# Two groups of TensorE transposes moved in a routed expert loop: gathered rows ahead of the last plain piece, gated rows behind the next turn's gate pieces

## What is computed

```python
combine = jnp.sum(jax.nn.one_hot(expert_id, N_EXPERTS) * weights[..., None], axis=1)   # 2 of 16 experts a token
for e in range(N_EXPERTS):
    he = jax.nn.silu(ht @ w_gate[e]) * (ht @ w_up[e])        # 1024 -> 512
    y = y + combine[:, e:e + 1] * (he @ w_down[e])           # 512 -> 1024
```

## Time and profile before

| | us |
|---|---|
| three runs of the kernel, median (lowest to highest) | 787.44 (785.16 to 789.09) |
| the profiled execution, its time | 787.38 |
| the profiled execution, its span | 785.5 |
| TensorE busy with matmuls | 751.7 |
| VectorE busy | 537.3 |
| ScalarE busy | 456.9 |
| GpSimd busy | 179.9 |

### The profile page before, as it was taken

The page is one execution under the profiler, slowest core; times in us unless marked ns, Lnnn a source line. Parts: engine busy times, 40 slices in busy tenths (PEclk is TensorE's granted clock), DMA queues, the critical chain, the costliest instruction groups (busy, mean ns, idle before and its releaser), DMA issues.

```text
span 785.5 us, 11565 instructions
## 1 busy us (share of the span) xinstructions
PE 751.7 (96%) x4124; PEld 582.1 (74%) x4124; DVE 537.3 (68%) x711; ACT 456.9 (58%) x665; POOL 179.9 (23%) x185
## 2 busy tenths in 40 slices
PE   4999999999999999999999969999999999999994
PEld 3978789777788889888788844677777777777763
DVE  5445378598782455622555488599989889899986
ACT  4455662487883236433443242587887887787862
POOL 3800023000001011000000100135555444555312
PEclk9999999999999999999999989999999999999997
DMA  9934521000405435542104768999999999999942
GB/s 297 233 94 141 155 83 59 1 2 2 161 3 188 134 108 177 172 151 66 53 1 143 310 236 321 398 380 381 383 370 373 382 372 375 380 384 384 385 154 107
DMA packets 61902, 166.88 MB, mean 212 GB/s; under 512 B 8224, under 2 KB 36192, under 8 KB 49576
## 3 DMA queue, kind: packets, MB, share of 16 engines
q1 hardware_dynamic: 56376, 150.69, 51.8%
q0 software_dynamic: 4480, 12.48, 6.8%
q10 hardware_dynamic: 1008, 3.21, 1.2%
HBM read 153.44 MB, written 12.85 MB: 212 GB/s over the span
## 4 chain that ended last, share of the span: by engine, by line
PE 93%; DVE 3%; DMA 1%; ACT 1%; issue 1%; POOL 0%; SPq 0%; POOLq 0%; ACTq 0%; DVEq 0%
PE ps L1976 24%; PE ps L1978 23%; PE ps L1977 23%; PE ps L2249 3%; PE ps L2197 3%; PE ps L2175 2%; PE ps L2444 2%; PE ps L2287 2%; PE ps L2178 1%; PE ps L2108 1%; PE ps L2424 1%; PE ps L2366 1%; DMA raw<-in_w_in 1%; PE ps L2179 1%; PE ps L2430 1%
## 5 line engine op out<-in xcount | busy, mean ns | idle before, releaser
L1356 DVE TENSOR_TENSOR wlo<-raw,whi 128x2048 fp32r<-128x2048 f32 x29 | 66.5, 2292 | 78.5 <-ACT whi L878 78.4
L1976 PE MATMUL ps<-whi,mhi 128*96 128x512 f32 (+1 forms) x276 | 110.1, 399 | 2.0 <-DVE mlo L1909 1.2
L1978 PE MATMUL ps<-whi,mlo 128*96 128x512 f32 (+1 forms) x276 | 109.3, 396 | 0.0
L1977 PE MATMUL ps<-wlo,mhi 128*96 128x512 f32 (+1 forms) x276 | 108.8, 394 | 0.0
L1371 DVE TENSOR_TENSOR wlo<-arena,whi 128x2048 fp32r<-128x2048 f32 x39 | 89.4, 2291 | 20.4 <-ACT whi L897 20.4
L741 POOL TENSOR_SCALAR stat<-stat 128x1 f32<-128x1 f32 x18 | 11.3, 630 | 355.9 <-ACT tok L903 209.4
L897 ACT ACTIVATE whi<-arena 128x2048 fp32r<-128x2048 f32 x39 | 74.7, 1915 | 26.4 <-PE ps L1978 26.4
L878 ACT ACTIVATE whi<-raw 128x2048 fp32r<-128x2048 f32 x29 | 55.4, 1910 | 48.5 <-PE ps L1978 48.4
L1976 PE MATMUL ps<-ahi,whi 128*128 128x512 f32 x192 | 75.6, 394 | 0.0
L1978 PE MATMUL ps<-ahi,wlo 128*128 128x512 f32 x192 | 74.8, 390 | 0.0
L1977 PE MATMUL ps<-alo,whi 128*128 128x512 f32 x192 | 74.8, 390 | 0.0
(11 more groups left out here) (396 smaller groups left out, 1692.4 us busy)
## 6 DMA issues: line engine op xcount, KB each, us to landing
arena<-in_exp_w_gate SPq DMA_DIRECT2D x30, 1024.0 KB, 14.4
arena<-in_exp_w_up SPq DMA_DIRECT2D x17, 1024.0 KB, 14.2
raw_a<-in_exp_w_down SPq DMA_DIRECT2D x16, 1024.0 KB, 15.2
raw<-in_exp_w_up SPq DMA_DIRECT2D x15, 1024.0 KB, 13.3
arena<-in_exp_w_down SPq DMA_DIRECT2D x9, 1024.0 KB, 18.6
raw<-in_exp_w_down SPq DMA_DIRECT2D x7, 1024.0 KB, 15.1
raw<-in_w_in SPq DMA_DIRECT2D x5, 1024.0 KB, 7.3
raw<-in_w_in SPq DMA_DIRECT2D x10, 512.0 KB, 5.6
```

What stands on the lines that cost most here:

```text
L1356: v.tensor_tensor(wlo[:, n % SPLIT, :], raw[:, n % RAW, :], whi[:, n % SPLIT, :].bitcast(F32), ALU.subtract).then_inc(lo_done, 1)
L1976: mm(out_, ahi_, bhi_, start=first, stop=False)
L1977: mm(out_, ahi_, blo_, start=False, stop=False)
L1978: return mm(out_, alo_, bhi_, start=False, stop=last)
```

## The change

On TensorE the row transposes of the entry stand ahead of plain piece 3, and those of the gated rows leave the entry and the end of the turn: they are issued behind the two gate pieces of the next turn, and once more behind the last turn. ScalarE's and VectorE's copies of the gated rows move with them, behind split 7 of the next turn, and in the entry VectorE's low copy of the rows goes ahead of `gated`.

```diff
@@ ScalarE, entry and turn @@
             xg_hi_out(2)
-            he_hi_out(1)
             act.wait_ge(route_done, 1)
...
                 split_expert(at + 7, h)
+                he_hi_out(j)
                 split_expert(at + 8, h)
                 silu(base + 2, j + 1)
...
                     y_out_half(1, base + 6)
-                if not last:
-                    he_hi_out(j + 1)
@@ VectorE, entry and turn @@
             split_expert(6)
+            xg_lo_out(2)
             gated(1, 4)
-            xg_lo_out(2)
-            he_lo_out(1)
             dve.wait_ge(route_done, 1)
...
-                for m in (7, 8, 9, 10):
+                split_expert(at + 7, h)
+                he_lo_out(j)
+                for m in (8, 9, 10):
                     split_expert(at + m, h)
                 gated(j + 1, RING * h + (at + 8), j)
...
                     split_expert(at + 12, h)
-                    he_lo_out(j + 1)
@@ TensorE, entry @@
                 pe.wait_ge(first_in, min(m, 1) + 1)
+                if m == 3:
+                    pe.wait_ge(xg_in, 16)
+                    xg_transposes()
...
-            pe.wait_ge(xg_in, 16)
-            xg_transposes()
-            pe.wait_ge(he_done, 2)
-            he_transposes()
             pe.wait_ge(route_done, 1)
@@ TensorE, turn and behind the last turn @@
                 pe.wait_ge(he_done, j + 1)
+                he_transposes()
                 for m in range(2):
                     pe.wait_ge(lo_done, n0 + 2 + m)
                     in_piece(ps[1], 6 + m, m)
...
                     down_piece(8 + m, m, 4)
-                pe.wait_ge(he_done, j + 2)
-                he_transposes()
...
             turn(turns + 1, True)
+            pe.wait_ge(he_done, turns + 3)
+            he_transposes()
             pe.wait_ge(he_lo, turns + 2)
```

## The result

The changed kernel takes 788.86 us (median of 22 runs, 787.89 to 790.29), the kernel before 787.70 on the same chips (22 runs, 785.16 to 789.19). The ratio is 1.002, 95% interval 1.0012 to 1.0028: the change makes the kernel 0.2% slower. The profiled execution took 789.06 us around a span of 787.2 (before: 787.38 and 785.5). The times of the kernel before fall into two groups with nothing between them: 6 of the 22 runs lie at 785.16 to 785.57 and the others at 787.18 to 789.19. In the runs beside the experiments the lower group has a mean granted clock of 0.991 and the upper one 0.987 to 0.989. Only one execution, of the upper group, has a trace, so which stop of the clock the lower group is spared is not shown. The changed kernel's 22 runs form one group.

The account below looks back on a forecast made before the run. TensorE, never idle in the expert loop, was taken as the bound, with idle stretches only at its entry. Entry gain -3.58 and loop loss +4.95 gave +1.37 us on 787.4: 788.7 us, range 784.0 to 791.2.

Parts of the forecast that it names:

- Gather's wait, row transposes, piece 3: Entry: wait of some 0.3 us, transposes 0.67, piece 3.44; first turn starts at 492.21, gain 3.58 us.
- Register load and branch code under piece 3, at nothing: Entry: TensorE's sequencer code ahead of the loop can run under piece 3's matmuls, costing nothing; bound above 0.47 us.
- Clock at full speed from turn 1 on: Entry: first gate piece runs at full clock, taking 2.84 us instead of 4.41.
- Rival C: Start of turn 1: clock stays at half speed, costing 1.57 us; 790.3 us; chance 0.08.
- Part 3, 15 x 0.33 = +4.95: Loop: moved gated-row transposes lengthen each of 15 turns by 0.33 us, while the boundary saving becomes a wait; 4.95 us lost.
- Rival A: Turn boundaries: wait hidden, turns keep 17.66 us, only the last turn's 0.33 lost; about 784.1 us; chance 0.14.
- ScalarE's copy between splits 7 and 8 is hidden: Turns: 0.49 us copy makes split 9 late by at most 0.1; 0.86 us idle ahead of split 10 covers it.
- rival B: ScalarE's queue in turns: the copy delays silu and later splits; 0.3 us more each gives 793.3 us; chance 0.09.
- The gather lands in time: Entry: first gather lands at 488.02, 5.4 us after issue; second near 499.5, ahead of its use at about 503.7.
- rival D: Entry: gather late or register code uncovered, giving 2 us instead of 3.6; 790.3 us; chance 0.09.
- The weights' pace (E): Loop: pace of weight loads, not TensorE, takes over; some 11 us of lead left late; no chance of its own.
- Behind the last turn, no change: End of the last turn: old order of down pieces, transposes and two copies, with 1.25 us of waiting, stays.

Follow-up runs that it names:

- experiment 3: Kernel before, with only the entry's row transposes ahead of plain piece 3 and their copy ahead of the gated multiply; 788.88 us, ratio 1.0007.
- experiment 5: Kernel before, with one instead of four transposes in each group of the gated rows; 787.91 us, ratio 1.0005.
- experiment 7: Kernel before, with TensorE's register load of the number of turns and its wait moved ahead of plain piece 3; 785.34 us, ratio 0.9977.
- experiment 4: Changed kernel, with the entry's row transposes behind plain piece 3 again, leaving only the loop's part; 790.34 us, ratio 1.0037 to the kernel before.
- experiment 1: Changed kernel, with VectorE's low copy of the gathered rows ahead of the gated multiply in every turn; 784.65 us, ratio 0.9962 to the kernel before.
- experiment 6: Changed kernel, with one instead of four transposes in each group of the gated rows; 784.43 us, ratio 0.9963 to the kernel before.
- Experiment 8: Changed kernel, low copy ahead of the gated multiply, entry's row transposes behind the first quarter of plain piece 3; 784.11 us, ratio 0.9956 to the kernel before.
- experiment 2: Kernel before, with VectorE's low copy of the gathered rows ahead of the gated multiply; 796.28 us, ratio 1.0117.

## Why the prediction was right

The forecast was 788.7 us, +1.37 on the profiled execution; measured was 788.86, +1.16 between medians and +1.18 by the account. Both terms came out smaller than forecast, the gain by 0.21 us and the loss by 0.40, and the two errors partly cancel. That the total is met to 0.2 us is in part luck; that each term is met to a tenth of its size or better is not. By its own steps:

- **Gather's wait, row transposes, piece 3** (-3.58 us as a sum): 3.37 were gained. The wait was 0.39 us for 0.3. The piece ended up 3.03 us long and not 3.44 (489.58 to 492.61), and the missing 0.4 came back on the first gate matmul, whose step is 0.64 us. The gate piece that was put at 2.84 us (its working, eleven steps of 0.23 and one of 0.29, gives 2.82) therefore took 3.17. The sum holds to 0.2 us, the terms less well.
- **Register load and branch code under piece 3, at nothing.** Turn 1's first matmul follows piece 3 with no idle time, so the code lies covered. But the prediction read the 0.73 us gap as the wait for the low copy, with at most 0.47 us for code behind it. Experiments 3, 5 and 7 show the code as what ended it: without the copy in the way the gap is 0.77 us, with a shorter group turn 1 starts no sooner, and without the register load the copy alone would have held it for 0.38. The bound of 0.47 holds only while the copy waits beside the code. The prediction reached the right sum because both go away together, which is luck in this term; the forecast of experiment 3, on the same reading, went wrong.
- **Clock at full speed from turn 1 on.** Right: 1.00. Rival C is out for the profiled execution. The Trainium skill (TensorE: Matmul & The Clock Gate, "Part 4: PE-mode transpose") says that transposes don't count as TensorE activity as matmuls do. By that rule an entry with a stop and eight transposes in it could have gone to half speed; the row shows 1.00. The runs don't refute the rule either: the stops that did cost clock were longer, 0.90 + 0.73 us before, 0.90 + 0.99 in experiment 5 and 1.19 + 0.77 in experiment 3, each around the gated group, and the 1.39 us of experiment 4 and 0.90 + 0.38 of experiment 7 cost none. Between the kernel before and experiment 7, a third of a microsecond of idle time at this place decided on 1.6 us. Each of these is one profiled execution.
- **Part 3, 15 x 0.33 = +4.95.** The mechanism is right, and shown by experiments 1, 5 and 6. The size is 4.55, because the price at a boundary was put too high. A turn of experiment 1, which has the group and no wait, lasts 17.67 us, and one of the changed kernel, which has both, 17.97. So what the boundary wait costs with its restart is 0.30 and not the 0.33 of the group that it replaces, and the group's own price is lost only in the last turn: 14 x 0.30 + 0.33 = 4.53. Rival A was on the right spot, and its turns of 17.66 us are what experiment 1 has (17.67) once the copy ends early enough.
- **ScalarE's copy between splits 7 and 8 is hidden.** Split 10 still has 0.86 us of idle time ahead of it (738.25): rival B is out.
- **The gather lands in time**: 5.6 us behind its issue; rival D is out for this execution. But its first half is near: in the profiled execution of experiment 1 the gather took 6.1 us, and TensorE waited 0.89 us for it. Experiment 8 has a later point, at which its execution shows no wait.
- **The weights' pace (E)** never released a split in the rows read; the gaps of the chain are named TensorE and ScalarE as before.
- **Behind the last turn, no change**: 1.25 us, as before.

Left open: how much of experiment 2's extra 0.3 us a turn is branch code and how much is wait handling, and why its two boundaries differ by 0.15 us. An experiment without that code would need the loop unrolled and wasn't made. Open too is which stop of the clock the lower group of the kernel before is spared, since no execution of that group was profiled.

## What to carry to other kernels

Work that stands in front of a held wait is free there as long as it ends first, and moving it costs nearly its full price (here 0.30 of 0.33 us) unless the wait moves as well: first ask which release the next step really hangs on and what is queued ahead of that on the releasing engine. Here one exchange in VectorE's queue, copy ahead of multiply, turned a change of +0.2% into one of -0.4%, and the same exchange without the change cost 1.2%, because then the multiply was the one that TensorE stood for: the two orders belong together. Keep register loads away from the place behind a wait that is held, and look there for other sequencer code, such as a loop's branch.

## What the runs showed of the hardware

- The first split matmul directly behind plain f32 matmuls has a step of 0.63 to 0.64 us to the next (492.61 to 493.25, and 492.53 to 493.16 in experiment 8), where one behind transposes has 0.28 to 0.30. Since the plain piece ahead of it seems short by about as much (3.03 us against 3.44), the plain matmuls' last work probably lies in this step; nothing here separates the two.
- The code of TensorE's sequencer shows in no busy time. The same register load cost nothing ahead of piece 3, and about a third of a microsecond, with the clock's fall behind it, after a held group of transposes (idle 0.73 us before, 0.38 in experiment 7). The profile puts such a gap down to "issue" (0.77 us in experiment 3) or to a copy that was done 0.5 us before (0.99 us in experiment 5).
- A group of four transposes costs TensorE 0.33 us in both places (742.85 to 743.41 less a step of 0.23, and 732.16 to 732.72 less the same step). Whether the kernel pays for it depended on whether the wait for the copy, worth 0.30 us, stood behind it.
